# Two stacked transformer blocks on one core: the next stage's first products start inside the closing stages

## The reference

```python
x = first_block(x, ...)      # gated mix of dilated and latent attention, then the MLP
    h = h + rms_norm(mix @ w_out, norm_mix_post)
    hn = rms_norm(h, norm_mlp_pre)
    ff = jnp.square(jax.nn.relu(hn @ w_ff1)) @ w_ff2             # 1024 -> 4096 -> 1024
    h = h + rms_norm(ff, norm_mlp_post)
return second_block(x, ...)  # four mixers (S5, HGRN2, FoX, mLSTM), then a gated MLP
    proj = rms_norm_2(h, ln_mix_pre) @ w_in
    h = h + rms_norm_2(mix @ w_out, ln_mix_post)
    a = rms_norm_2(h, ln_ffn_pre)
    ff = (silu(a @ w_ffn_gate) * (a @ w_ffn_up)) @ w_ffn_down    # 1024 -> 2816 -> 1024
    h = h + rms_norm_2(ff, ln_ffn_post)
```

## Time and profile before

| | |
|---|---|
| median of 3 runs | 1734.03 us (1734.02 to 1734.77) |
| the profiled execution | 1732.92 us, its span 1731.1 us |
| mean granted clock | 0.932 |
| TensorE matmuls | 1577.9 us busy (91%) |
| VectorE | 829.0 us (48%) |
| ScalarE | 560.6 us (32%) |
| POOL | 261.6 us (15%) |
| DMA | 129.24 MB, mean 75 GB/s |

### The profile page before, as it was taken

How to read it: one execution, slowest core, us unless ns; L and a number is a source line. 1 busy time by engine, 2 the same in 40 slices (tenths; PEclk the granted TensorE clock), 3 DMA queues, 4 the chain that set the end, 5 groups by cost and what they waited for, 6 DMA issues and landing times. The chain is left out here.

```text
span 1731.1 us, 18563 instructions
## 1 busy us (share of the span) xinstructions
PE 1577.9 (91%) x7456; PEld 1278.5 (74%) x7456; DVE 829.0 (48%) x1213; ACT 560.6 (32%) x848; POOL 261.6 (15%) x275
## 2 busy tenths in 40 slices
PE   7988899669989899999997999999769899999997
PEld 6876788557767688888886766775767788888886
DVE  4232443356654454434346786564854433333434
ACT  4222334324452432323234322454223422212212
POOL 0000000000021698000002276200321100000000
PEclk9999899789999999999998999995759999999998
DMA  4222011220022222222231222020002222222222
GB/s 164 97 77 97 29 69 62 74 74 1 1 73 86 75 96 98 98 97 98 97 122 58 73 74 73 31 74 1 1 1 73 98 97 95 95 96 95 96 83 88
DMA packets 36458, 129.24 MB, mean 75 GB/s; under 512 B 4580, under 2 KB 20860, under 8 KB 24212
## 3 DMA queue, kind: packets, MB, share of 16 engines
q1 hardware_dynamic: 36084, 127.93, 21.6%
q10 hardware_dynamic: 288, 0.12, 0.0%
HBM read 124.82 MB, written 3.17 MB: 74 GB/s over the span
## 5 line engine op out<-in xcount | busy, mean ns | idle before, releaser
L223 DVE TENSOR_TENSOR ring_lo<-ring_raw,ring_hi 128x2048 fp32r<-128x2048 f32 (+3 forms) x115 | 266.2, 2318 | 225.0 <-ACT ring_hi L213 224.9
L242 PE MATMUL bank<-xT_hi,ring_hi 128*128 128x512 f32 (+2 forms) x864 | 342.2, 396 | 5.3 <-PEq L1316 3.7
L242 PE MATMUL bank<-xT_lo,ring_hi 128*128 128x512 f32 (+2 forms) x864 | 339.6, 393 | 0.0
L242 PE MATMUL bank<-xT_hi,ring_lo 128*128 128x512 f32 (+2 forms) x864 | 339.1, 392 | 0.0
L213 ACT CAST ring_hi<-ring_raw 128x2048 fp32r<-128x2048 f32 (+3 forms) x115 | 212.7, 1852 | 269.4 <-DMA ring_raw<-in_w_ff 131.1
L242 PEld LDWEIGHTS bank<-xT_hi,ring_hi 128*128 128x128 f32 (+2 forms) x864 | 163.3, 189 | 46.5 <-issue 11.6
L242 PEld LDWEIGHTS bank<-xT_hi,ring_lo 128*128 128x128 f32 (+2 forms) x864 | 163.2, 189 | 35.9
L242 PEld LDWEIGHTS bank<-xT_lo,ring_hi 128*128 128x128 f32 (+2 forms) x864 | 163.4, 189 | 34.7
L242 PE MATMUL bank<-ring_hi,hid_hi 128*128 128x512 f32 x432 | 169.3, 392 | 4.0 <-DVE ring_lo L223 4.0
L242 PE MATMUL bank<-ring_lo,hid_hi 128*128 128x512 f32 x432 | 169.0, 391 | 0.0
L242 PE MATMUL bank<-ring_hi,hid_lo 128*128 128x512 f32 x432 | 168.8, 391 | 0.0
(11 more groups left out here) (443 smaller groups left out, 2203.0 us busy)
## 6 DMA issues: line engine op xcount, KB each, us to landing
ring_raw<-in_w_ff SPq DMA_DIRECT2D x32, 1024.0 KB, 4.7
ring_raw<-in_w_up SPq DMA_DIRECT2D x22, 1024.0 KB, 4.8
ring_raw<-in_w_proj SPq DMA_DIRECT2D x8, 1024.0 KB, 5.1
ring_raw<-in_w_gates SPq DMA_DIRECT2D x8, 1024.0 KB, 4.8
ring_raw<-in_w_out SPq DMA_DIRECT2D x8, 1024.0 KB, 4.8
ring_raw<-in_w_fm SPq DMA_DIRECT2D x12, 512.0 KB, 4.8
ring_raw<-in_w_dn_a SPq DMA_DIRECT2D x6, 1024.0 KB, 4.8
ring_raw<-in_w_proj SPq DMA_DIRECT2D x8, 512.0 KB, 4.4
```

What stands on the lines that cost most here:

```text
L223: k.nc.vector.tensor_tensor(k.ring.lo[:, g % SLOTS, 0:n], k.raw[:, g % SLOTS, 0:n], plain(k.ring.hi[:, g % SLOTS, 0:n]), ALU.subtract).the ...
L242: mm = k.nc.tensor.matmul(out, x, y, start=first and n == 0, stop=last and n == 3 * len(pairs) - 1)
```

## The change

Three closings (mix1, mlp1, mix2) get a list of the next stage's first tiles (`ahead`): two tiles, one tile, two tiles. After the products of token tile 3, TensorE waits for the next chunk and for the low parts of token tile 1, and makes the first of these tiles for tokens 0 to 255 (`begin`), then the transposes of token tile 2, then the second tile for tokens 0 to 255 (where there are two), then the transposes of tile 3. The S5 transposes now come after those, and use the bank of tile 2. Then TensorE waits for all low parts and makes both tiles for tokens 256 to 511. The next stage skips these tiles (`begun`). To keep banks 0 and 1 free for them, tile t and column half c now use bank 2t + c. In the first MLP the first two chunks each hold two output tiles over all eight feature tiles instead of four over four, loaded in two pieces. No product is left out.

```diff
--- before.py
+++ after.py
@@ -509,7 +509,7 @@
 
 
 def stage_gemm(k, steps, evac, owner=None, act_each=None, dve_each=None, dve_tail=None, pool=None,
-               needs=(), closing=None, opening=None):
+               needs=(), closing=None, opening=None, begun=0):
 
 
 
@@ -548,6 +548,9 @@
         def _(pe):
             seen = set()
             for i, (g, j, out, pairs, first, last) in enumerate(steps):
+                if i < begun:
+
+                    continue
                 if opening is not None and i < T:
                     opening.pe(pe, i)
                 if g not in seen:
@@ -1010,10 +1013,12 @@
 
 
 
-    def __init__(self, k, tag, g, lhs, phases, gain_name, at, pre=None, part=None, needs=None, out=None, aside=None):
+    def __init__(self, k, tag, g, lhs, phases, gain_name, at, pre=None, part=None, needs=None, out=None, aside=None,
+                 ahead=None):
         self.k, self.first, self.lhs, self.phases, self.pre = k, g, lhs, phases, pre
         self.end = g + 2 * len(phases)
         self.part, self.needs, self.out, self.aside = part, needs or {}, out, aside
+        self.ahead, self.ahead_done = ahead or ((), None)
         self.gain_row = k.d[gain_name]
         self.gain = k.sb(f"cl_gain_{tag}", at[0], [P, D])
         self.z = k.sb(f"cl_z_{tag}", at[1], [P, D])
@@ -1028,7 +1033,7 @@
              "gain", "weighed"))
 
     def bank(self, t, c):
-        return self.k.pb[4 * c + t]
+        return self.k.pb[2 * t + c]
 
     def cols(self, c):
         return slice(512 * c, 512 * c + 512)
@@ -1097,7 +1102,7 @@
                 for t in range(T):
                     if p == 0 and held:
 
-                        pe.wait_ge(*held[4 * c + t])
+                        pe.wait_ge(*held[2 * t + c])
                     mm = product(p, t, c, p == 0, False)
                 mm.then_inc(k.w_used.sem, 1)
         for c in range(2):
@@ -1110,12 +1115,29 @@
                 if self.pre is not None and t >= 2 and c == 0:
                     turn(t - 2)
         if self.pre is not None:
-            turn(2)
+            half = S // 2
+            if self.ahead:
+
+                wait_chunk(k, pe, self.end)
+                pe.wait_ge(self.low.sem, self.low.base + 4)
+            for n in range(2):
+                if n < len(self.ahead):
+                    self.begin(n, 0, half)
+                turn(2 + n)
             if self.aside is not None:
 
-                pe.wait_ge(self.low.sem, self.low.base + 2)
-                self.aside.turn(pe, self.bank(0, 0))
-            turn(3)
+                pe.wait_ge(self.low.sem, self.low.base + 6)
+                self.aside.turn(pe, self.bank(2, 0))
+            if self.ahead:
+
+                pe.wait_ge(self.low.sem, self.low.base + 8)
+            for n in range(len(self.ahead)):
+                self.begin(n, half, S).then_inc(self.ahead_done.sem, 1)
+
+    def begin(self, n, a, b):
+
+        _, _, out, pairs, _, _ = self.ahead[n]
+        return products(self.k, out[:, a:b], [(x, y[:, a:b]) for x, y in pairs], True, True)
 
     def square_y(self, act, t, c):
 
@@ -1180,7 +1202,7 @@
         if norm:
             self.high_part(act, 3)
             if self.aside is not None:
-                self.aside.keep(act, self.bank(0, 0))
+                self.aside.keep(act, self.bank(2, 0))
 
     def pool(self, pool):
         k, g = self.k, self.k.nc.gpsimd
@@ -1581,8 +1603,9 @@
     summed.base += KD
     high.base += KD
     k.s5_in = S5Inputs(k)
+    begun, _, _ = gemm(k, g + 4, KD, 8, feature_tiles(k.xT, (0, P), 2 * P), 0)
     g = stage_closing(k, Closing(k, "mix1", g, lambda f, t: mixT[:, f, t * P:(t + 1) * P], FULL_DEPTH, "norm_mix_post",
-                                 (104, 108, 112, 116, 120), pre=0, aside=k.s5_in))
+                                 (104, 108, 112, 116, 120), pre=0, aside=k.s5_in, ahead=(begun, k.sig("gemm_done"))))
 
 
     H = FF1 // P // MLP1_PARTS
@@ -1593,7 +1616,12 @@
     steps, j, needs, tile = [], 0, {}, []
     for part in range(MLP1_PARTS):
         f0 = j
-        for _ in range(H // 4):
+        for n in range(H // 4):
+            if part == 0 and n == 0:
+                for _ in range(2):
+                    s, j, g = gemm(k, g, KD, 8, feature_tiles(k.xT, (0, P), 2 * P), j)
+                    steps += s
+                continue
             s, j, g = gemm(k, g, KD, 4, feature_tiles(k.xT, range(0, 512, P), 512), j)
             steps += s
         tile += [("up", part, f) for f in range(H)]
@@ -1608,8 +1636,9 @@
     ra, rr = k.sig("relu_done"), k.sig("relu_read")
     up = [i for i, x in enumerate(tile) if x[0] == "up"]
     taken = k.sig("gemm_free_dve").base
+    begun2, _, _ = gemm(k, g + 4, KD, 8, feature_tiles(k.xT, (0,), 96, m=96), 0, range(4))
     closing = Closing(k, "mlp1", g, lambda f, t: hid[:, f, t * P:(t + 1) * P], FULL_DEPTH, "norm_mlp_post",
-                      (152, 120, 124, 156, 104), pre=1, part=y,
+                      (152, 120, 124, 156, 104), pre=1, part=y, ahead=(begun2, k.sig("proj2_done")),
                       needs={(0, 0): (k.sig("gemm_free_dve").sem, taken + up[-5] + 1),
                              (1, 0): (k.sig("gemm_free_dve").sem, taken + up[-1] + 1)})
 
@@ -1630,7 +1659,7 @@
         return nc.vector.tensor_tensor(hid.lo[:, f, :], r2[:, n % 2, :], plain(hid.hi[:, f, :]), ALU.subtract)
 
     stage_gemm(k, steps, evac_ff, lambda j: "both" if tile[j][0] == "up" else "dve", needs=needs,
-               pool=s5_powers(k, er, ei, 166), closing=closing)
+               pool=s5_powers(k, er, ei, 166), closing=closing, begun=len(begun))
     k.g = closing.end
     k.s5_powers = er, ei
     return None
@@ -1714,8 +1743,9 @@
     ycT = k.split("ycT", 104, [P, KD, S], 120)
     stage_turn(k, [([k.ycat[:, t, f * P:(f + 1) * P] for t in range(T)], P, ycT[:, f, :], col(k, "mix_gain2", f))
                    for f in range(KD)])
+    begun, _, _ = gemm(k, g + 4, KD, 8, feature_tiles(k.xT, (0, P), 2 * P), 0)
     g = stage_closing(k, Closing(k, "mix2", g, lambda f, t: ycT[:, f, t * P:(t + 1) * P], FULL_DEPTH, "ln_mix_post_2",
-                                 (152, 156, 160, 164, 168), pre=2))
+                                 (152, 156, 160, 164, 168), pre=2, ahead=(begun, k.sig("gemm_done"))))
 
 
     hid = k.split("hid2", 104, [P, FF2_PARTS[0], S], 128)
@@ -1781,7 +1811,7 @@
                                     ALU.subtract).then_inc(low.sem, 1)
 
     stage_gemm(k, steps, evac_glu, lambda j: "both" if tile[j][0] == "gate" else "dve", act_each=high_part,
-               dve_each=low_part, needs=needs, closing=closing)
+               dve_each=low_part, needs=needs, closing=closing, begun=len(begun))
     return None
 
 
@@ -2020,6 +2050,9 @@
 
             seen = set()
             for i, (c, j, out, pairs, start, last) in enumerate(steps):
+                if i < 1:
+
+                    continue
                 if c not in seen:
                     seen.add(c)
                     n = c - first - 2
@@ -2841,7 +2874,10 @@
                     ("w_out", 4)):
         whole(name, (0, 2, 1, 3) if name == "w_out" else range(n))
     for q in range(MLP1_PARTS):
-        whole("w_ff1", range(4 * q, 4 * q + 4))
+        if q == 0:
+            for half in range(2):
+                add_weights(k, *columns_of(d, "w_ff1", (0, 1), 4, 512, 256 * half, 256 * half + 256))
+        whole("w_ff1", range(4 * q + (2 if q == 0 else 0), 4 * q + 4))
         first = 8 * (q // 2) + 2 * (q % 2)
         at = (0, 1, 4, 5) if q < MLP1_PARTS - 1 else (0, 4, 1, 5)
         whole("w_ff2", [first + i for i in at])
```

## The result

| | before | changed |
|---|---|---|
| median | 1734.03 us (5 runs, 1733.96 to 1736.92) | 1742.79 us (5 runs, 1737.45 to 1743.37) |
| the profiled execution | 1732.92 us | 1737.45 us, its span 1735.7 us |
| mean granted clock | 0.932 | 0.933 |

The ratio is 1.0040 (95% interval 1.0024 to 1.0057): slower by 0.4%. The forecast was 1736.3 us in a range of 1730 to 1740.5, so the time lies 2.3 us above the range. The profiled execution of the changed kernel is the shortest of its five; the other four took 1742.31 to 1743.37 us.

A forecast was written before the change was run, and what follows sets the result against it. TensorE, busy 91% of the span, was taken as the bound, with idle and slow-clock time at three seams. Terms -0.4 + 2.7 + 0.0 = +2.3 us on the 1734.03 us median gave 1736.3 us, range 1730 to 1740.5.

The forecast's parts named there:

- second halves: Products for tokens 256 to 511, waiting for the last low parts ahead of the stage boundary; 5.76 us for two halves.
- pause of 4.8 us: After the second halves TensorE stands still at each seam: 0.16 us last result, 0.33 boundary, 4.3 chunk split.
- The 2.1 us that I added for every restart: Mean cost of TensorE's slow first products at the low clock, added after the pause at each of three seams.
- seam 1: From closing mix1 into the first MLP: new 593.4 against old 593.8, so -0.4 us.
- seam 3: From closing mix2 into the second MLP: new and old both 1369.6, so 0.0 us.
- The rule cited with the pause: Skill's clock rule that bursts with waits between them start slow; said to speak against the change, changing no figure.
- The side sum by the Trainium skill's steps: With skill steps of 0.109 and 0.216 us, a half would cost 2.6 us and the forecast fall by 1.3 us.
- Seam 2's term: From closing mlp1 into the second block's projection: +1.4 or +4.0 us by when the clock falls; middle +2.7 taken.
- a late tile 1 moves all that follows: In the second block's projection, delay of tile 1 is not hidden, since input products at 966.99 wait for that chain.
- The faster one: Rival: clock stays at 2.4 GHz or split runs during second halves, 2.1 us better per seam; 1728.7 us, chance 0.15.
- The slower one: Rival: clock falls before the second halves and again in the pause; +3.6 to +7.8 us, middle 1739.7, chance 0.33.
- What was put at no cost: Recut of first MLP chunks (under 1 us late without cover), banks by tile, POOL's S5 powers starting 6 us later.

The follow-up runs named there:

- e1: The changed kernel run once more, unedited: 1741.96 us, ratio 1.0044 to the kernel before.
- e5: The changed kernel with early products after closing mix1 alone, taken out at the other two closings: 1733.14 us, ratio 0.9991 to the kernel before.
- e7: The changed kernel with early products after closing mix2 alone, taken out at the other two closings: 1735.19 us, ratio 1.0001 to the kernel before.
- e8: The changed kernel plus 18 matmuls of 512 columns, results never read, in each of the three pauses: 1731.98 us, ratio 0.9986 to the kernel before.
- e6: The changed kernel with early products after closing mlp1 alone, taken out at the other two closings: 1738.72 us, ratio 1.0036 to the kernel before.
- e4: The changed kernel with the next stage's second chunk split inside the closing, not at the head of the next block: 1721.70 us, ratio 0.9924 to the kernel before.
- e2: The kernel before with only the banks by tile (2t + c): 1735.03 us, ratio 1.0003 to the kernel before.
- e3: The changed kernel without any early products, keeping banks by tile, recut chunks and later S5 transposes: 1736.59 us, ratio 1.0011 to the kernel before.
- e9: e4 with early products and early split taken out after closing mlp1, kept at the other two closings: 1723.26 us, ratio 0.9927 to the kernel before.
- e11: The changed kernel plus nine matmuls, results never read, in the projection ahead of its wait for POOL: 1739.42 us, ratio 1.0023 to the kernel before.

## Why the prediction was wrong

**The seams were right.** First halves in idle time at the full clock; second halves behind the low parts, 580.7 to 586.5 us forecast, 580.19 to 586.0 measured; pause of 4.8 us forecast from the end of the last step, 4.79 measured (4.91 from the start of the last product to the start of the next) at each seam; clock at 0.50 at all three restarts in the shorter execution. In e1 it was still full at the restarts of seams 1 and 3 and fell 0.5 and 0.3 us behind them. The 2.1 us that I added for every restart fit in the mean alone: in the shorter execution they were about 2.8, 2.0 and 1.4 us (14, 10 and 7 products, each 0.2 us slower). TensorE restarts at seam 1 at 590.83 us, forecast 591.3. By the stretches, seam 1 is worth +0.5 and -0.7 us (changed, and again; forecast -0.4), seam 3 -0.5 and -0.2 (forecast 0.0), and the profiles of the one-seam kernels agree (-0.3 in e5, -0.2 in e7). The rule cited with the pause (the Trainium skill, TensorE: Matmul & The Clock Gate, "HAM oscillation — how this bites in real kernels": bursts with waits between them start slow each time) agrees with these traces, but for those first tenths in e1. And e8 prices it: with the clock held up, the same pauses cost 10 us less, 4.5 of them at the seams. The side sum by the Trainium skill's steps (same page, "Back-to-back issue gap", 0.109 and 0.216 us) is off: it takes the shorter step for the new halves alone. Taken for the 89 old products as well (89 x 0.012 = 1.1 us), it moves the forecast by 0.2 us, not 1.3.

**Seam 2's term was too small.** It measured +2.9 us in the shorter execution and +4.5 in the longer, +4.2 alone (e6). I had taken the middle of +1.4 and +4.0. The upper end was the better one, since in all three profiles the clock fell before the second half. In the shorter one it fell only just before (low from 945.1, the half from 945.36) and was full again for the end of the half.

**The step that failed** is the sentence behind it, "a late tile 1 moves all that follows": I priced what follows seam 2 as moved, at its old length. It is not carried along unchanged. Of the 6.5 us by which e1's growth over before (8.8) exceeds the forecast's 2.3, the term of seam 2 holds 1.8, this one 5.2, and the other two seams take 0.5 back. In the projection TensorE waits a second time, for VectorE's and POOL's work on the second S5 unit. That wait is in the trace of before, 1.37 us, and I had not looked there. Where that wait was 2.01 us and more (e4, e1, e6) the clock fell, and the next 10 to 14 us ran at 0.50: +4 us from the first s_cT to FoX in e1 and e4. Where it was up to 1.95 us (before, the shorter execution, e2, e3, e5, e7, e8, e9) it did not. Taking the wait and with it the fall away (e11) takes away the longer executions and 3 us of median. That the length of the wait alone decides is not shown, since no run moved the wait without changing its length. Just ahead of inject TensorE waits 2.2 us for ScalarE in all fourteen profiles (2.24 to 2.25); the clock is low at inject or within 3 us behind its start in thirteen of them, and in e6 it stays full:

```profile
971.89 1.98 PE L2039 MATMUL bank<-fm,s_bT 32*128 32x512 f32 x4 [2.24 <-ACT fm L2016]
```
```profile
969.50:983.00 13.50, 11.26 (x45) 8.29 (x45) 11.28 (x11) 4.73 (x5) 2.83 (x2) 1.00 0.25 79
```

Why the wait for POOL grows can be read from the same rows: the chain of VectorE and POOL starts from the inject products, while TensorE reaches the wait sooner or later by how much of its work behind them runs at the low clock. Before, the four inject products took 3.03 us, the last of them slow, and the wait ended 46.1 us after their start; in e1 they took 3.78 us, all slow, and it ended 46.9 us after it; TensorE was ready after 44.8 us in both. In the shorter execution they took 1.98 us, and the numbers are 45.1 and 43.2. In e6, with no slow product behind inject at all, the numbers are 45.1 and 42.1, the longest wait. The inject products before and in e1:

```profile
966.99 3.03 PE L2009 MATMUL bank<-fm,s_bT 32*128 32x512 f32 x4 [2.25 <-ACT fm L1986]
```
```profile
970.48 3.78 PE L2039 MATMUL bank<-fm,s_bT 32*128 32x512 f32 x4 [2.24 <-ACT fm L2016]
```

So where the low clock falls around inject, which shifts with everything ahead of it, seam 2 included, moves the wait by 1 us and more, and the slow stretch behind it costs 4 us or not. This account of the wait's length comes from rows alone; no run varied it by itself.

**The rivals.** The faster one was to come from a clock that stays up or a split that runs with the second halves; neither is in the change as it was made. As a price it was far too low: e4 makes it real, and it is worth 20 us against the changed kernel, not 7.6, because it removes the pauses as well as the slow starts. The slower one had the right seam, from +3.6 us on, and a chance of 0.33: at seam 2 the clock did fall ahead of the second half and again in the pause, at seams 1 and 3 it did not. Its middle, 1739.7 us, lacks the 4 us downstream. The range ended at 1740.5 because no case held a cost outside the seams.

**What was put at no cost.** The banks (e2) show none. With the recut and the later S5 transposes (e3) the time is 0.3 to 3.3 us above before; I had said nothing, and under 1 us if the cover were gone. That term may have been short by up to those 3 us, but the intervals of e2 and e3 overlap, and the profile of e3 shows the extra time where e2's does, behind inject.

## What to carry to other kernels

Work that is moved ahead of a barrier takes its cover with it: the chunk split behind the barrier was free as long as 5 to 11 us of products could hide it, and became a pause of 4.6 us and a slow restart once these were done early. Move what the next stage needs next along with it (here two lines, 20 us). And when a change shifts a stage by a few microseconds, look at every wait that TensorE already has in the stages behind: here one of 1.37 us that had cost only itself became one of 2.16 us with 4 us of slow products behind it.

## What the runs showed of the hardware

A wait of 2.01 us amid dense work was followed by the low clock in e4, one of 1.95 us at the same place was not in e8: 0.06 us apart, 4 us or nothing. The eleven profiles with this wait are too few to call that a threshold, and the wait of 2.24 us ahead of inject, with the low clock in thirteen profiles and without it in e6, speaks against one by length alone. The clock's low stretch at one and the same place also had different lengths: at seam 2 without early products it lasted 10 us in the kernel before (940.5 to 950.7) and 14 us in e9 (934.5 to 948.2), with the same instructions there. And useless matmuls in a pause paid for themselves: with 54 of them, all in time that was idle, a kernel of 1742 us took 10 us less.
